# Second and last feed-forward tile with 512 moving columns instead of 256

## The reference, cut to what matters

```python
for l in range(2):                                  # first block, per layer
    x = x + 0.5 * swiglu(rms_norm(x, ffa_norm[l]), ffa_w_in[l], ffa_w_out[l])
    ... mixer (three branches, gates) ...
    x = x + 0.5 * swiglu(rms_norm(x, ffb_norm[l]), ffb_w_in[l], ffb_w_out[l])
# then, twice: x = x + mixer(...);  x = x + conv_glu_ffn(rmsnorm(x, ...), ...)

def swiglu(h, w_in, w_out):                         # 1024 -> 2 x 2816 -> 1024
    gate, up = jnp.split(h @ w_in, 2, axis=-1)
    return (jax.nn.silu(gate) * up) @ w_out

def conv_glu_ffn(h, w_gate, w_up, conv_w, conv_b, w_down):
    g = causal_dwconv_2(h @ w_gate, conv_w) + conv_b   # 3 taps over the tokens
    return (jax.nn.silu(g) * (h @ w_up)) @ w_down
```

## Time and profile before

| | |
|---|---|
| median of three runs | 1927.32 us |
| profiled execution, its own time | 1927.81 us |
| its span | 1926.0 us |
| busy: TensorE, its weight loads, VectorE, ScalarE, GpSimd | 1918.8, 1716.1, 1467.5, 1086.9, 84.8 us |
| granted TensorE clock | full in all 40 slices |

### The profile page before, as it was taken

How to read it: one execution, slowest core, us unless ns; L and a number is a source line. 1 busy time by engine, 2 the same in 40 slices (tenths; PEclk the granted TensorE clock), 3 DMA queues, 4 the chain that set the end, 5 groups by cost and what they waited for, 6 DMA issues and landing times.

```text
span 1926.0 us, 34607 instructions
## 1 busy us (share of the span) xinstructions
PE 1918.8 (100%) x12889; PEld 1716.1 (89%) x12889; DVE 1467.5 (76%) x2279; ACT 1086.9 (56%) x1701; POOL 84.8 (4%) x61
## 2 busy tenths in 40 slices
PE   9999999999999999999999999999999999999999
PEld 8888999999888888889999998889898888888888
DVE  6777887767777777778777777777577888888887
ACT  6555764664555555557546644555355656675654
POOL 0000012010000000000110102000000000110000
PEclk9999999999999999999999999999999999999999
DMA  6656552344555655555424455555745655545654
GB/s 234 198 189 199 168 175 89 121 154 153 165 190 191 196 172 189 191 180 186 143 90 148 139 168 164 196 190 184 223 158 172 196 188 191 168 127 161 200 189 142
DMA packets 95222, 331.02 MB, mean 172 GB/s; under 512 B 10896, under 2 KB 15632, under 8 KB 94992
## 3 DMA queue, kind: packets, MB, share of 16 engines
q1 hardware_dynamic: 92992, 325.64, 52.6%
q10 hardware_dynamic: 2128, 3.94, 0.6%
HBM read 327.91 MB, written 1.64 MB: 171 GB/s over the span
## 4 chain that ended last, share of the span: by engine, by line
PE 96%; DVE 2%; ACT 1%; DMA 1%; issue 0%; SPq 0%; ACTq 0%; DVEq 0%
PE ps L2185 94%; PE ps L2211 1%; DVE w_lo L1236 1%; PE ps L2453 1%; DMA raw<-stream 1%; PE ps L2680 0%; ACT w_hi L562 0%; DVE a_both L1289 0%; PE ps L2836 0%; PE ps L2620 0%; PE ps L2808 0%; DVE tmp L2045 0%; ACT arena L789 0%; PE ps L2568 0%; PE ps L2204 0%
## 5 line engine op out<-in xcount | busy, mean ns | idle before, releaser
L2185 PE MATMUL ps<-a_both,w_hi 128*128 128x256 f32 (+1 forms) x4512 | 930.6, 328 | 1.0 <-DVE a_both L1289 0.7
L1236 DVE TENSOR_TENSOR w_lo<-raw,w_hi 128x1024 fp32r<-128x1024 f32 x614 | 749.9, 1227 | 235.1 <-ACT w_hi L562 234.3
L2185 PEld LDWEIGHTS ps<-a_both,w_hi 128*128 128x128 f32 x4512 | 759.6, 190 | 80.3 <-issue 2.8
L562 ACT ACTIVATE w_hi<-raw 128x1024 fp32r<-128x1024 f32 x614 | 637.1, 1053 | 142.2 <-DMA raw<-stream 97.3
L2185 PE MATMUL ps<-a_both,w_lo 128*128 128x256 f32 x3168 | 610.6, 283 | 0.0
L2185 PE MATMUL ps<-w_hi,a_both 128*128 128x512 f32 (+2 forms) x1792 | 563.5, 384 | 0.3
L2185 PEld LDWEIGHTS ps<-a_both,w_lo 128*128 128x128 f32 x3168 | 490.6, 191 | 8.9
L2185 PEld LDWEIGHTS ps<-w_hi,a_both 128*128 128x128 f32 x1792 | 333.9, 188 | 63.4 <-DVE a_both L1347 0.8
L2185 PE MATMUL ps<-w_lo,a_both 128*128 128x512 f32 (+2 forms) x896 | 343.1, 383 | 0.0
L2185 PEld LDWEIGHTS ps<-w_lo,a_both 128*128 128x128 f32 x896 | 169.0, 189 | 26.8
L635 ACT ACTIVATE a_both<-arena 128x256 fp32r<-128x256 f32 x132 | 55.3, 419 | 142.9 <-DVE arena L1342 100.0
(11 more groups left out here) (335 smaller groups left out, 1239.1 us busy)
## 6 DMA issues: line engine op xcount, KB each, us to landing
raw<-stream SPq DMA_DIRECT2D x613, 512.0 KB, 3.5
arena<-upad SPq DMA_DIRECT2D x8, 284.0 KB, 5.8
gates<-late ACTq DMA_DIRECT2D x1, 1088.0 KB, 8.3
out<-tmp SPq DMA_DIRECT2D x3, 256.0 KB, 2.4
upad<-arena ACTq DMA_DIRECT2D x2, 288.0 KB, 8.4
con<-consts SPq DMA_DIRECT2D x1, 560.0 KB, 5.4
raw<-stream ACTq DMA_DIRECT2D x1, 512.0 KB, 3.9
x<-x_in SPq DMA_DIRECT2D x2, 256.0 KB, 5.3
```

The costliest lines, as they stand in the source:

```text
L562: nc.scalar.activation(w_hi[:, u % SLOTS, :], raw[:, u % RAW, :], ACT.Copy).then_inc(hi_ready, 1)
L1236: V.tensor_tensor(w_lo[:, u % SLOTS, :], raw[:, u % RAW, :], w_hi[:, u % SLOTS, :], ALU.subtract).then_inc(split_ready, 1)
L2185: return nc.tensor.matmul(o, a, b, start=start, stop=stop, **k)
```

## The change

Tile 1 of all six feed-forwards, and tile 21 of A0, B0, A1 and B1, go by `fm_wide`. Tile 21 of C0 and C1 stays narrow. On ScalarE these tiles get a `low_half`, and on VectorE `added` and `scaled` stand in the place of `scaled_narrow`. The units, their order and the DMAs are as before. `first_stat` and the spread are handed to `fm_wide`: the first stands between the two units' `w_hi` passes, the second in the middle of the first unit's `w_lo` pass.

```diff
         def wide_tiles(F):
-            return (FT - 3) * (F // FT) + F % FT - 1
+            n = F // FT
+            return (FT - 2) * n + min(n, 2 * DEPTH) + F % FT
+
+        def tile_end(f):
+            return 2 * f + 2 if f < 2 else 3 * f - (f == FT - 1)
...
                 def tile(f, splits, j=0):          # ScalarE
                     F, p = F0 + f, f % 2
-                    if 1 < f < FT - 1:
-                        low_half(p, n0 + 3 * f, j)
+                    if 0 < f < (FT - 1 if conv else FT):
+                        low_half(p, n0 + tile_end(f), j)
...
                 def tile(f, splits, j=0):          # VectorE
-                    F, p, wide = F0 + f, f % 2, 1 < f < FT - 1
+                    F, p, wide = F0 + f, f % 2, 0 < f < (FT - 1 if conv else FT)
                     if wide:
                         added(p, wide_tiles(F), j)
                     else:
-                        scaled_narrow(p, n0 + (3 * f - 1 if f > 1 else 2 * f + 2))
+                        scaled_narrow(p, n0 + tile_end(f))
...
-            def fm_wide(u, b, j=0):
+            def fm_wide(u, b, j=0, first=None, middle=None):
                 for q in range(2):
+                    if first and q:
+                        first()
...
                     for k in range(KC):
+                        if middle and (q, k) == (0, KC // 2):
+                            middle()
...
                 def gate_up(f, u, j=0):            # TensorE
-                    if f < FT - 1:
+                    if f < FT - 1 or F0 < 2 * DEPTH * FT:
                         fm_wide(u, 4 + 2 * p, j)
...
-                fm(n0 + 2, bank(6, 0, TOK), middle=None if t else first_stat)
-                fm(n0 + 3, bank(6, TOK, 512), middle=lambda: ffn_spread(t))
+                fm_wide(n0 + 2, 6, first=None if t else first_stat, middle=lambda: ffn_spread(t))
```

## The result

The kernel after takes **1932.72 us** in the median of 11 runs (1931.15 to 1934.36), the kernel before 1927.32 in as many (1926.64 to 1927.95). The ratio is 1.0026, with a 95% interval of 1.0019 to 1.0034: slower by 5.4 us in the medians. A second series gave 1932.32 (8 runs) and 1.0027 (1.0016 to 1.0037). The profiled execution took 1931.66 us, which is among the lowest of the 11, with a span of 1929.9, 3.85 us more than before's. I forecast 1930.0 and gave 1925.8 to 1932.0 as the range. The sign of the sum was right, the size too small, and the median lies 0.7 us above the range.

The account below looks back on a forecast made before the run. TensorE, with 96% of the chain, was taken to bound the kernel. -0.2 + 0 + 2.0 + 0.2 + 1.6 - 0.8 = +2.8, say +2.7, on 1927.81 us, median 0.49 lower, gave 1930.0 us; 8-in-10 range 1925.8 to 1932.0.

Parts of the forecast that it names:

- The pair: Each of ten pairs: wide 5.54 us against narrow 5.76, 16 weight loads and starts fewer, a gain of 0.22 us.
- B0: First tiles of B0: all splits in time even with TensorE 0.22 us earlier, so -0.22 us.
- A1: First tiles of A1: TensorE waits for the diagonal, which hangs on the feed-forward before; it waits longer, so 0.
- last tiles: Tile 21 of A0, B0, A1, B1: gain stays with almost nothing to spare, 4 x -0.2 = -0.8 us.
- B1: First tiles of B1: GpSimd holds up n+7's split, later units come late, tile 4 starts late: +2.0 us, no pair's gain.
- its own terms 1.3, 0.2, 0.5 and 0.1: At B1's entry, how late units n+8, n+9, n+10 and n+11 are split: 1.3, 0.2, 0.5 and 0.1 us.
- A0, C0, C1: First tiles: late n+10 and n+11 splits less the pair's gain; A0 +0.16 us, C0 and C1 +0.8 each.
- rival B: C0 and C1: convolution tiles can't catch up after the first late split; +5.8 us on top, 1935.8 us; chance 0.14.
- Rivals A: All entries: nothing is late, splits still arrive in time; -1.8 us, 1925.5 us; chance 0.16.
- C: Pairs: 512-column matmuls cost 0.131 us, not 0.227, so each pair saves 1.5 us more; 1915 us; chance 0.02.
- D: Pairs get shorter and only B1 is late: +2.0 - 1.4 = +0.6 us, 1927.9 us; chance 0.16.
- = +2.8 us, say +2.7, on 1927.81 us of the profiled execution: Whole kernel: sum of the changed places, added to the profiled execution; median 0.49 lower, forecast 1930.0 us.

Follow-up runs that it names:

- b_plus64: Kernel before, eight warm-up matmuls ahead of A0 replaced by 24 of one column, 64 TensorE instructions more: 1930.75 us, ratio 1.0016.
- a_minus32: Kernel after, with the warm-up ahead of A0 packed in 32 TensorE instructions fewer: 1931.79 us, ratio 1.0021.
- b_ kernels: Kernel before, only the warm-up packed in 32 or 16 TensorE instructions fewer, 32 or 64 more: 1928.35, 1927.48, 1929.11, 1930.75 us.
- x_both: Kernel after, with VectorE scaling tile 1 ahead of the split of unit n+7 and GpSimd's tap products of B1 held back: 1926.78 us, ratio 0.9997.
- x_both_minus32: Kernel after with tile 1 scaled before unit n+7's split, B1's tap products held back, warm-up 32 TensorE instructions fewer: 1926.37 us, ratio 0.9996.
- b_minus32: Kernel before, only the warm-up ahead of A0 packed in 32 TensorE instructions fewer: 1928.35 us, ratio interval 0.9995 to 1.0013.

## Why the prediction was wrong in size

- *The pair.* Forecast -0.22, measured -0.19 (5.76 to 5.57 us for tile 21 of A0). The 0.03 between them came from the earlier trace rows: I set tile 20's pair, which a further pair follows, against tile 21's, which a down follows. By the rule of the Trainium skill that I weighed ("TensorE: Matmul & The Clock Gate", Back-to-back issue gap) it would have been an estimated 0.04. The trace disagrees with that, and the section itself calls the formula the gap of an isolated matmul.
- *B0, A1, last tiles.* B0 and the last tiles are right: -0.16, and -0.19 each, of which the downs behind give 0.02 to 0.08 back in every kernel with a wide tile 21, and 0.00 in those without. So the cover that I counted there was just used up. A1 shows -0.22 against 0, but this stretch is at -0.18 to +0.11 in the kernels whose tile 1 is narrow, so that the wide tile can't be credited with it. I had it hang on the end of the feed-forward before. In fact the diagonal stands on VectorE behind a split that waits for a load: ScalarE stood still 1.84 us for it in before and 1.61 in after.
- *B1.* Right in size (+2.0, though its own terms 1.3, 0.2, 0.5 and 0.1 add up to 2.1; measured +2.12), one stop missed: tile 3 first waits 0.9 us for `scaled` of tile 1, behind the held-up split. I had let it start unchanged and put all on n+8. In the sum it is the same, since n+8 was the later of the two.
- *A0, C0, C1.* Right: +0.20, +0.82, +0.78 against +0.16, +0.8, +0.8. As forecast, the stop is ahead of tile 4 and gone thereafter: the rest of C0's tiles shifts by 0.00, which leaves nothing of rival B. Rivals A, C and D fall with the measured waits, the 0.19 of a pair, and C0.
- *The step that failed.* "= +2.8 us, say +2.7, on 1927.81 us of the profiled execution": it took all that is not changed as standing still, and gave it no term. The miss of 2.7 us is made of 0.1 in the sum of the changed places, 1.1 in the rest of the trace (mixer 1's +0.93 by the fetch, the remainder unfollowed), and 1.5 in the step from the profiled execution to the median. I had put the median 0.49 below it as in before, and it lies 1.06 above it. The 0.49 was no constant: over the 14 kernels with a trace the median lies between 0.87 below the profiled execution (b_plus64) and 1.10 above it (a_minus32).
- *The cause of that last part stays open.* The 11 runs of after spread over 3.2 us, those of before over 1.3 (but over 2.8 in 33 runs on another chip). Medians without a trace can't be taken apart. That one load or another is hit in some executions and not in others would fit, but it was only argued.
- *The range* had bounds for every priced step and no width for the place of the fetches, which by the b_ kernels is worth -0.1 to +1.9 us (b_plus64 less the 1.3 of its start, an estimate from one trace) with no change at all.

x_both has the change without its costs, and is 0.5 us below the median before (0.8 against the runs on its own chip), which can't be told from none. By its shifts the four last tiles and five of the six tiles 1 give 1.7 us (A1 gives nothing), and B1's own 0.6 are gone besides; mixer 1's +1.22 takes half of that back. The lowest median is that of x_both_minus32, which can't be told from x_both's either. Without that mixer's shift it shows 2.3 us less than before in the trace, and 1.2 in the median.

## What to carry to other kernels

The wider matmul paid only for the weight loads and starts that it saved (here 0.19 us for 16), so look first at what its longer path through the other engines makes late: an operation added ahead of a split shifts each split behind it. Order those engines' work so that what unblocks the next engine comes first, and keep GpSimd's SBUF work away from places without lead. And where an effect is to be told to 0.2%, run a null variant that changes only the number of instructions: its spread is the floor below which a change of code can't be credited or blamed. Look at the granted clock of the null variant as well, as b_plus64 shows.

## What the runs showed of the hardware

- **Code fetches delay weight loads.** A packet of the code queue is 16 KB (1.18 MB in 72 packets). In stretches of narrow matmuls they come some 15 us apart (889.2, 903.9 and 918.9 us before). At the two places followed in mixers 0 and 1, one that starts 0.9 to 2.3 us after the issue of a 512 KB load makes it land 0.9 to 1.4 us later (4.1 to 4.7 us in place of 3.3), though the packet itself is 3% of its bytes. The load before had landed there, and the next was issued 1.1 us behind. At 2.5 us and more it has no effect at these places. The Trainium skill ("Runtime: NRT & Kernel Launch", Instruction fetch mechanics) has blocks of 16 KiB, 256 instructions, fetched ahead over a queue, and calls the cost mostly hidden. The block size agrees: 256 instructions are 128 loads with their matmuls, at 0.120 us an estimated 15.4 us. That the cost is hidden holds for TensorE itself: in before and after none of its stops of over 0.15 us comes within 3 us behind the start of a fetch. It does not hold for the loads beside it.
- **32 instructions are some 2 us of phase.** The fetch that is at 218.4 us in before comes at 220.9 in b_minus32, and after's at 884.4 comes at 886.0 in a_minus32.
- **A GpSimd product beside VectorE.** In B1 the split of n+7 takes 2.33 us with GpSimd's product beside it and 1.22 without, while `added`, which reads PSUM for one operand, takes 0.68 and 0.69.
- **The clock after a pause.** In b_plus64 the granted clock is 0.50 (1.2 GHz) from 7.7 to 11.1 us, after a warm-up that ended 0.9 us sooner than in before and 2.0 us of idle TensorE in place of 0.7. The starts of its matmuls of 256 columns are 0.21 us apart in that stretch, and 0.13 in before.
